# Branch and output projections of a hybrid decoder step: eight block products replaced by seven, with resident split weights and GpSimd sums

## The reference

```python
    h = h * jax.nn.sigmoid(o_pre) * jax.nn.silu(z_m)
    y_m = h @ w_proj_m
    cv, conv1 = short_conv(c_g * x_c, conv0, conv_w)
    y_c = (jax.nn.silu(z_c) * b_g * cv) @ w_proj_c
    mix = jax.nn.sigmoid(g_m) * y_m + jax.nn.sigmoid(g_c) * y_c
    out = x + mix @ w_out
```

## Time and profile before

| | |
|---|---|
| median of 3 runs (lowest, highest) | 2363.55 us (2358.3, 2364.69) |
| profiled execution, span from first to last instruction | 2356.7 us |
| TensorE busy | 2323.1 us, 99% |
| VectorE, ScalarE, GpSimd busy | 1488.1, 948.6, 77.5 us |
| mean granted TensorE clock | 0.998 |

### The profile page before, as it was taken

One profiled execution on the slowest core, in us unless ns is written; L12 is line 12 of the kernel. 1 busy time (PEld: TensorE's weight loads), 2 busy tenths in 40 slices (PEclk: granted clock), 3 DMA queues, 4 the chain that ended last, 5 costly groups with the idle time before them and its releaser, 6 DMA issues. The chain is left out here.

```text
span 2356.7 us, 41040 instructions
## 1 busy us (share of the span) xinstructions
PE 2323.1 (99%) x14643; PEld 2254.8 (96%) x14643; DVE 1488.1 (63%) x2703; ACT 948.6 (40%) x1717; POOL 77.5 (3%) x84
## 2 busy tenths in 40 slices
PE   8999999999999999999999999999999999999998
PEld 8998999999999999999999999999998999998886
DVE  4447788898876687777776677777755333324333
ACT  3224444444454444455655444555554101002121
POOL 0011000000110000000020000000000000000000
PEclk9999999999999999999999999999999999999999
DMA  6665655455775765656765766557567433443442
GB/s 224 209 215 136 199 187 181 157 177 176 232 220 174 232 202 184 191 159 195 240 191 177 235 202 195 188 175 217 176 185 260 156 102 110 138 143 126 138 138 86
DMA packets 424977, 425.66 MB, mean 181 GB/s; under 512 B 32810, under 2 KB 363690, under 8 KB 424870
## 3 DMA queue, kind: packets, MB, share of 16 engines
q1 hardware_dynamic: 424870, 424.25, 56.9%
HBM read 297.36 MB, written 126.85 MB: 180 GB/s over the span
## 5 line engine op out<-in xcount | busy, mean ns | idle before, releaser
L1658 PE MATMUL b_g<-x_hi,w_hi 128*128 128x344 f32 (+1 forms) x3024 | 985.5, 326 | 9.0 <-DVE rows L1333 4.3
L1658 PE MATMUL b_g<-x_lo,w_hi 128*128 128x344 f32 (+1 forms) x3024 | 967.9, 320 | 0.0
L1658 PE MATMUL b_g<-x_hi,w_lo 128*128 128x344 f32 (+1 forms) x3024 | 967.0, 320 | 0.0
L1658 PEld LDWEIGHTS b_g<-x_hi,w_hi 128*128 128x128 f32 x3024 | 569.3, 188 | 16.1 <-DVE rows L1333 4.4
L1658 PEld LDWEIGHTS b_g<-x_lo,w_hi 128*128 128x128 f32 x3024 | 569.3, 188 | 1.7
L1658 PEld LDWEIGHTS b_g<-x_hi,w_lo 128*128 128x128 f32 x3024 | 569.4, 188 | 0.0
L1155 ACT ACTIVATE w_hi<-w_operands 128x512 fp32r<-128x512 f32 x519 | 323.5, 628 | 272.9 <-PE b_g L1658 261.2
L1295 DVE TENSOR_TENSOR w_lo<-w_operands,w_hi 128x512 fp32r<-128x512 f32 x519 | 354.2, 695 | 1.2
L1155 ACT ACTIVATE w_hi<-stages 128x512 fp32r<-128x512 f32 x216 | 134.7, 629 | 138.3 <-PE b_g L1658 119.4
L1295 DVE TENSOR_TENSOR w_lo<-stages,w_hi 128x512 fp32r<-128x512 f32 x216 | 145.6, 684 | 7.7 <-ACT w_hi L1155 6.9
L2017 PE MATMUL c_g<-act_hi,RH 128*128 128x294 f32 x448 | 134.4, 300 | 2.1 <-DVE rows L1948 2.1
(11 more groups left out here) (305 smaller groups left out, 3116.0 us busy)
## 6 DMA issues: line engine op xcount, KB each, us to landing
w_operands<-w_in SPq DMA_DIRECT2D x282, 256.0 KB, 5.2
stages<-w_ops_d SPq DMA_DIRECT2D x36, 768.0 KB, 5.5
w_operands<-w_ops_d SPq DMA_DIRECT2D x34, 768.0 KB, 4.9
stages<-w_in SPq DMA_DIRECT2D x72, 256.0 KB, 3.8
w_operands<-w_ops_d SPq DMA_DIRECT2D x70, 256.0 KB, 6.3
w_ops_d<-w_operands SPq DMA_DIRECT2D x18, 768.0 KB, 3.3
w_ops_d<-stages SPq DMA_DIRECT2D x18, 768.0 KB, 3.4
w_ops_d<-w_operands SPq DMA_DIRECT2D x36, 256.0 KB, 3.9
```

Of the source, the lines that this page charges most:

```text
L1658: last = nc.tensor.matmul(bank[:, 0:n], w[:, j, k, :], x[:, k, 0:n], start=(j < 4 and k == 0 and m == 0), stop=(k == 3 and m == 2), skip_g ...
```

## The change

`phase_c` and `phase_d` are rewritten to the seven-product scheme. In `phase_c` the unit is a *pair*: one quarter `p` (of 4) of the output channels, as two blocks of 128 (`p` and `p`+4), times one tile of 2 x 258 tokens. 2 branches x 4 tiles x 4 quarters give 32 pairs, numbered n = 16 x branch + 4 x tile + p. A pair has 7 products, each 4 x 3 matmuls of 258 columns. Each pair alternates between two sets of four banks; products 5, 6 and 7 go on top of banks 0, 2 and 3 after ScalarE or VectorE has read them.

The weights are 12 *blocks* (4 quarters of each matrix). A block is loaded raw (`load_raw`, four transfers of 256 KB), three operands are sums (four instructions, `weight_sum`), and it is split in four pieces (`COARSE`; seven for the first and last block, `FINE`) by `split_high` on ScalarE and `split_low` on VectorE. Four blocks are resident (`WH`, `WL`), block b in slot b % 4. `AHEAD` says in which pair a block is split, `RAW_AT` in which its load is issued. `POOL_SUMS` is all of `AHEAD`: GpSimd makes the sums of all blocks but the first (made by VectorE at the end of `phase_b`) and, in its own block of code, of the last one. There is one raw buffer and one buffer for sums for blocks 0 to 8.

The activations of a tile are loaded as four quarters, GpSimd makes four sums (`act_sum`, 1032 elements a partition), ScalarE and VectorE split seven operands (`act_high`, `act_low`) during the last pair of the tile before. A pair's result is 128 x 2 x 516: ScalarE and VectorE gather it from PSUM (`step`) and one VectorE instruction applies the gate (`gate`). Branch m is stored to `mix_d`; branch c is added to it in DRAM by accumulating transfers which GpSimd issues (`accumulate`). `head_norm_w` is now multiplied into the z row in `phase_b`. `phase_d` takes tiles of 256 tokens with 84 matmuls of 512 columns, and the 8 samples in 48 matmuls with plain quarters of the same weights. The old bodies of both phases are left out here:

```diff
...
-TN = 294
-NTC = 7
-TP = TN * NTC
+TN = 258
+NG = 4
+TP = 2 * TN * NG
+NPAIR = 4 * NG * 2
+NT2 = L // (2 * P)
+STORED = [0, 4, 1, 5, 2, 3, 6]
+COARSE = [(2, 4), (0, 2), (4, 6), (6, 7)]
+FINE = [(0, 1), (4, 5), (1, 2), (5, 6), (2, 3), (3, 4), (6, 7)]
+SUMS_OF = {(0, 1): 0, (4, 5): 2, (1, 2): 3, (5, 6): 1, (2, 3): 0, (3, 4): 0, (6, 7): 4, (2, 4): 0, (0, 2): 3, (4, 6): 2}
+NW = 12
+BANK = (0, 1, 2, 3, 0, 2, 3)
...
+def load_raw(eng, g, b):
+    w, c0, c1 = weight_block(g, b)
+    w = w[0].rearrange("(k p) n -> p k n", p=P)
+    for j, (k0, c) in enumerate(((0, c0), (0, c1), (4, c0), (4, c1))):
+        eng.dma_start(raw_buffer(g, b)[:, j], w[:, k0:k0 + 4, c:c + P]).then_inc(raw_signal(g, b)[0], 16)
+def weight_sum(eng, engine, g, b, at):
+    r, e = raw_buffer(g, b), sum_buffer(g)
+    if at == 0:
+        engine.wait_ge(*raw_signal(g, b))
+        if b:
+            engine.wait_ge(g.w_ready, pieces_before(b))
+        eng.tensor_tensor(e[:, 1], r[:, 1], r[:, 3], ALU.add).then_inc(g.w_sum, 1)
+    elif at == 1:
+        engine.wait_ge(g.w_sum, 4 * b + 1)
+        eng.tensor_tensor(e[:, 0], e[:, 1], r[:, 0], ALU.subtract).then_inc(g.w_sum, 1)
+    elif at == 2:
+        eng.tensor_tensor(r[:, 1], r[:, 0], r[:, 1], ALU.subtract).then_inc(g.w_sum, 1)
+    else:
+        engine.wait_ge(g.w_sum, 4 * b + 2)
+        eng.tensor_tensor(e[:, 2], r[:, 2], e[:, 0], ALU.subtract).then_inc(g.w_sum, 1)
...
+def split_high(nc, act, g, b, at):
+    lo, hi = chunks(b)[at]
+    act.wait_ge(*raw_signal(g, b))
+    if SUMS_OF[lo, hi]:
+        act.wait_ge(g.w_sum, 4 * b + SUMS_OF[lo, hi])
+    nc.scalar.activation(g.WH[:, b % 4, lo:hi], piece(g, b, lo, hi), ACT.Copy).then_inc(g.w_hi, 1)
+def split_low(nc, dve, g, b, at):
+    lo, hi = chunks(b)[at]
+    dve.wait_ge(g.w_hi, pieces_before(b) + at + 1)
+    nc.vector.tensor_tensor(g.WL[:, b % 4, lo:hi], piece(g, b, lo, hi), g.WH[:, b % 4, lo:hi].bitcast(F32),
+                            ALU.subtract).then_inc(g.w_ready, 1)
...
+def act_sum(nc, pool, g, s, at):
+    a, b, c, d, e = (act_block(g, s, slot) for slot in range(5))
+    if at == 0:
+        pool.wait_ge(*act_signal(g, s))
+        if s:
+            pool.wait_ge(g.x_ready, 7 * s)
+        nc.gpsimd.tensor_tensor(b, c, b, ALU.subtract).then_inc(g.xq_sum, 1)
+    elif at == 1:
+        pool.wait_ge(g.xq_sum, 4 * s + 1)
+        nc.gpsimd.tensor_tensor(d, b, a, ALU.add).then_inc(g.xq_sum, 1)
+    elif at == 2:
...
-                        nc.scalar.activation(ZT[:, 0:n], ER[:, q, 1, 0:n], ACT.Tanh, scale=0.5).then_inc(z_set, 1)
+                        nc.scalar.activation(ZT[:, 0:n], ER[:, q, 1, 0:n], ACT.Tanh, scale=0.5)
+                        nc.scalar.activation(ER[:, q, 1, 0:n], ER[:, q, 1, 0:n], ACT.Copy,
+                                             scale=g.hnw[:, bass.ds(2 * i + q, 1)]).then_inc(z_set, 1)
...
+                        if extra == "end" and q == 1 and 2 <= j < 6:
+                            weight_sum(nc.vector, dve, g, 0, j - 2)
...
+    AHEAD = {0: 1, 1: 2, 2: 3, 13: 4, 14: 5, 16: 6, 17: 7, 29: 8, 30: 9, 31: 10}
+    RAW_AT = {0: 1, 1: 2, 2: 3, 4: 4, 14: 5, 15: 6, 17: 7, 18: 8, 28: 9, 30: 10, 31: 11}
+    POOL_SUMS = {n: b for n, b in AHEAD.items()}
...
+            def raw_weights(b):
+                if b <= 8:
+                    sp.wait_ge(g.w_ready, pieces_before(b - 1) + (2 if b > 1 else 6))
+                elif b == 10:
+                    sp.wait_ge(g.w_ready, pieces_before(8) + 2)
+                elif b == 11:
+                    sp.wait_ge(g.w_ready, pieces_before(9) + 2)
+                load_raw(sp, g, b)
+            load_tanh(0)
+            raw_weights(1)
...
+            for n in range(NPAIR):
+                s = n // 4 + 1
+                if n:
+                    load_tanh(n)
+                    if n <= NPAIR // 2:
+                        store(n - 1)
+                if n == 1:
+                    for par in range(2):
+                        sp.wait_ge(g.row_out[par], g.rows_stored[par])
+                if n % 4 == 0:
+                    sp.wait_ge(g.x_ready, 7 * s)
+                    if s == 2 * NG:
+                        for par in range(2):
+                            sp.wait_ge(g.acc_out[par], 32)
+                    load_acts(sp, g, s)
+                if n in RAW_AT and n:
...
+            def accumulate(n):
+                pool.wait_ge(gated, n + 1)
+                pool.dma_start(two_rows(g.mix_d, n), MX[n % 2], accum_op=ALU.add).then_inc(g.acc_out[n % 2], 16)
+            for n in range(NPAIR):
+                if n == NPAIR // 2:
+                    for par in range(2):
+                        pool.wait_ge(mix_out[par], 16 * NPAIR // 4)
+                if n > NPAIR // 2:
+                    accumulate(n - 1)
+                if n % 4 == 2:
+                    act_sum(nc, pool, g, n // 4 + 1, 0)
+                    act_sum(nc, pool, g, n // 4 + 1, 1)
+                if n in POOL_SUMS:
+                    for at in range(4):
+                        weight_sum(nc.gpsimd, pool, g, POOL_SUMS[n], at)
+                if n % 4 == 3:
+                    act_sum(nc, pool, g, n // 4 + 1, 2)
+                    act_sum(nc, pool, g, n // 4 + 1, 3)
+            accumulate(NPAIR - 1)
...
+            for j in range(NOP):
+                split_high(nc, act, g, 0, j)
+                act_high(nc, act, g, 0, j)
+                if j == 3:
+                    for br in range(2):
+                        row = g.ER[:, 1, br, 0:2 * PASSES[2][1]]
+                        nc.scalar.activation(row, row, ACT.Tanh, scale=0.5).then_inc(last_tanh, 1)
+            def step(n, j):
+                act.wait_ge(done, 7 * n + j + 1)
+                bank = G[4 * (n % 2)][:, 0:TN]
+                if j == 0:
+                    if n:
+                        act.wait_ge(ev, 5 * (n - 1) + 1)
+                    nc.scalar.activation(P1[:, :], bank, ACT.Copy).then_inc(copied, 1)
+                elif j == 4:
+                    row_free(act, n)
+                    nc.scalar.activation(MX[n % 2][:, 0, 0:TN], bank, ACT.Copy).then_inc(copied, 1)
+            for n in range(NPAIR):
+                for j in range(NOP):
+                    step(n, j)
+                    if n in AHEAD and j >= 3:
+                        split_high(nc, act, g, AHEAD[n], j - 3)
+                    if n % 4 == 3:
+                        act_high(nc, act, g, n // 4 + 1, j)
...
+            def gate(n):
+                dve.wait_ge(ev, 5 * n + 5)
+                dve.wait_ge(copied, 2 * n + 2)
+                dve.wait_ge(tg_in, 16 * (n + 1))
+                nc.vector.scalar_tensor_tensor(out=MX[n % 2], in0=TG[:, :, :], scalar=1.0, in1=MX[n % 2],
+                                               op0=ALU.add, op1=ALU.mult).then_inc(gated, 1)
+            def ahead(b, at):
+                if at in (2, 3) and b not in POOL_SUMS.values():
+                    weight_sum(nc.vector, dve, g, b, 2 * at - 4)
+                    weight_sum(nc.vector, dve, g, b, 2 * at - 3)
+                elif 4 <= at < 7:
+                    split_low(nc, dve, g, b, at - 4)
+                elif at == 7:
+                    split_low(nc, dve, g, b, 3)
+            for j in range(NOP):
+                split_low(nc, dve, g, 0, j)
+                act_low(nc, dve, g, 0, j)
+            for n in range(NPAIR):
+                for j in range(NOP):
+                    if j == 0:
+                        if n - 1 in AHEAD:
+                            ahead(AHEAD[n - 1], 7)
+                        if n and n % 4 == 0:
+                            act_low(nc, dve, g, n // 4, NOP - 1)
+                        if n:
+                            gate(n - 1)
+                    step(n, j)
+                    if n in AHEAD:
+                        ahead(AHEAD[n], j)
+                    if n % 4 == 3 and j:
+                        act_low(nc, dve, g, n // 4 + 1, j - 1)
+            gate(NPAIR - 1)
+            ahead(AHEAD[NPAIR - 1], 7)
+            act_low(nc, dve, g, 2 * NG, NOP - 1)
...
+            for n in range(NPAIR):
+                br, t, p = place(n)
+                for j in range(NOP):
+                    if t == 0:
+                        pe.wait_ge(g.w_ready, pieces_for(4 * br + p, j))
+                    if p == 0:
+                        pe.wait_ge(g.x_ready, 7 * (n // 4) + j + 1)
+                    if j == 0 and n > 1:
+                        pe.wait_ge(copied, 2 * (n - 1))
+                    elif j == 1 and n > 1:
+                        pe.wait_ge(ev, 5 * (n - 2) + 1)
+                    elif j == 2 and n > 1:
+                        pe.wait_ge(ev, 5 * (n - 2) + 4)
+                    elif j == 3 and n > 1:
+                        pe.wait_ge(ev, 5 * (n - 2) + 5)
+                    elif j == 4:
+                        pe.wait_ge(copied, 2 * n + 1)
+                    elif j == 5:
+                        pe.wait_ge(ev, 5 * n + 2)
+                    elif j == 6:
```

(8 more changed lines are left out.)

721 lines of the change are left out of this document (354 added, 367 removed).

## The result

| | before | after |
|---|---|---|
| median of 4 runs of each | 2361.03 us | 2440.52 us |
| lowest to highest | 2358.3 to 2364.69 | 2439.87 to 2443.41 |
| profiled execution, span | 2356.7 us | 2438.9 us |

The ratio is 1.0339 (95% interval 1.0325 to 1.0354): the changed kernel is slower by 79.5 us, where +16 was forecast and +38 was the range's end. Sign right, size wrong by a factor of five.

What follows compares the result with a forecast made beforehand. TensorE, busy 99% of the span, was taken as the bound. With waits the pair stage goes from 374.9 to 413.3 us (+38.4), the output stage saves 22.3: +16, a median of 2380 us, range 2350 to 2402.

Steps and rivals of the forecast that it cites:

- Tile changes 1.6 each: Pair stage, pairs 8, 12, 20, 24, 28: the sixth product waits for VectorE's second PSUM sum, 8 us together.
- the sides allow it: Output stage: VectorE's work fits beside each 19.5 us tile, so 96 fewer matmuls save the full 22.3 us.
- The first pairs: Pair stage's start: pairs 1 to 3 wait for weight loads, sums and splits; pair 4 starts at 83.0 us.
- Then 8.4 for the load: Pairs 2 and 3: tanh rows, a mix store and a weight block queued together need 8.4 us with their issues.
- Pairs 14 to 18: Pair stage: blocks 5 and 7 load in the pair that splits them, GpSimd holds block 6's sums; 21.8 us lost.
- barrier 0.8: Between pair and output stages: 0.8 us for the barrier, within 15.1 from the last pair matmul's end to the next.
- Pair 31 itself loses 1.8: Last pair of the pair stage: a loss of 1.8 us, counted beside the 15.1 us border.
- Costed at nothing: Input stage: z row scaling on ScalarE (24 copies, about 0.7 us each) and first block's sums (4 x 0.6) add nothing.
- Rivals 1: Pair stage: GpSimd's blocking costs almost nothing and waits are shorter; -14 us for the kernel, chance 0.24.
- 4: Rival with full gain, all weight block turnarounds hidden: -68 us over both stages, chance 0.02, counted within the faster rival's.
- rival 2: Whole kernel: gain and waits both halve, time within 0.3% (7 us) of before; chance 0.15.
- Rival 3: Pair stage from pair 18: accumulating transfers over 13 us hold up row buffers; at 16 us +21 more, chance 0.09.

Runs made afterwards that it cites:

- e1: Changed kernel with the output stage's activation loads issued one tile earlier on SP, ahead of the load of x and the store; 2421.9 us.
- e9: Changed kernel with raw blocks 1 to 3 and 5 to 7 loaded where their low parts will stand, and blocks 5 to 7 split later; 2402.2 us.
- e13: e9 with GpSimd's weight sums ahead of its wait for branch m's stores and of the accumulating transfer; 2390.2 us.
- e5: Changed kernel with GpSimd's sums for a pair, from pair 4 on, waiting until TensorE has finished the pair before; 2436.7 us.
- e3: Changed kernel with the last accumulating transfer issued as GpSimd's first instruction of the output stage, behind the barrier; 2436.4 us.
- e11: Changed kernel without the scaling of the z rows by the head norm weight (24 ScalarE copies); 2436.6 us, one run.
- e6: Changed kernel with the first weight block's four sums behind the last product of the last input pair on VectorE; 2439.9 us.
- e12: Changed kernel with the edits of e1, e3 and e9 together, all weight sums and the pair stage's activation sums on VectorE; 2334.1 us.
- e8: Changed kernel with weight sums and activation sums (all but the first block's and first group's) on VectorE instead of GpSimd; 2394.1 us.
- e14: e12 with the weight sums of blocks 1 to 11 back on GpSimd, ahead of the accumulating transfers; 2339.2 us.
- e7: Changed kernel with all 16 accumulating transfers made plain stores by the same queue; 2433.8 us, one run.
- e10: Changed kernel with only the activation sums (all but the first group's) on VectorE, weight sums staying on GpSimd; 2412.8 us.

## Why the prediction was wrong

**Right by its steps.** Starts of 258-column matmuls 0.120 us apart and of 512-column ones 0.233 (medians). Low parts beside GpSimd 3 us and more (up to 4.2). Tile changes 1.6 each: 1.9 (pairs 8, 24, 28), though pair 4, a tile change too, was left out of the list (1.8). VectorE ends 12.1 us after the last pair matmul: 12.3.

**The step that failed most** is "the sides allow it: a tile lasts 19.5 us, VectorE's part is ... 12 us, plus 5 us of blocking". It weighs VectorE's work against the tile and never follows when the next tile's activations land. 17 us of work in 19.5 doesn't fit if 6.8 us of it is spent before a load, with the needed sum behind it. The stage took 196.9 us for 176.1, 20.8 more; with the load early it takes 175.8 (e1). It is the largest term, and alone would have put the forecast at +37.

**The first pairs: right mechanism, partly by luck.** Pairs 1 to 4 at 28.5, 47.4, 71.2, 83.0: measured 29.3, 53.2, 75.4, 88.2. "Then 8.4 for the load" was mis-sized: block 2 landed 11.3 us after the gate of pair 0, block 3 10.1 us after that of pair 1. (The 11.4 us from which the 8.4 is worked out is a median; the transfer of the earlier trace rows itself took 11.8, with a fourth one issued behind it.) And the two activation sums that the prediction puts in front of block 3's ran earlier, beside block 2's low part:
```profile
1838.38 3.44 DVE L254 TENSOR_TENSOR proj_lo<-stages,proj_hi 128x1024 fp32r<-128x1024 f32 x1 [3.19 <-ACT proj_hi L248]
```
So pair 2 comes 5.0 us later than forecast and pair 3, counted from pair 2, 1.6 us earlier: part of the nearness of 75.4 to 71.2 is two errors that cancel.

**Pairs 14 to 18: right mechanism, size off.** "Gate of pair 13 at 1.9, so block 5 has landed at 10.3": the gate ended 6.9 us into pair 14, the block landed at 17.9. GpSimd's activation sums, written for pair 14 and begun 3.3 us before it, held up block 4's low parts (3.2 and 3.1 us for 1.2), and the load took 11.0 us from the gate, not 8.4. Pair 15 lost 15.5 and not 7.5. The reading that GpSimd holds the next sums until the stores have landed was right (e9, e13).

**GpSimd's order taken for its time.** The prediction lets a sum happen in the pair for which it is written. GpSimd has no other work and runs ahead: block 4's sums, written for pair 13, met the low parts of pair 11 (5.7 us at pair 12, e5).

**"VectorE ends 12.1 us after the last matmul; barrier 0.8":** the barrier took 5.9, for the last transfer (e3: 0.3 without it). **"Pair 31 itself loses 1.8":** it lost 6.6. TensorE stood there behind the copy and the second sum of its own pair:
```profile
2213.31 0.39 PE L2166 MATMUL c_g<-act_hi_b,proj_hi 128*128 128x258 f32 x1 [2.18 <-ACT c_part L2057]
2217.32 0.58 PE L2166 MATMUL c_g<-act_hi_b,proj_hi 128*128 128x258 f32 x1 [1.73 <-DVE c_part L2086]
```
The prediction had seen that GpSimd's sums stand there behind an accumulating transfer, and priced it too low: with them ahead of it pair 31 loses 0.1 us (e13, from 6.1 in e9). **"Costed at nothing"** were the z copies (about 3 us, e11, one run; ScalarE's idle share is an average and doesn't say what waits behind a copy) and the first block's sums, hidden as work but not as a wait for their load (3 us, of which e6 shows that it only moves).

**The clock was priced once, and is paid at each wait.** After the 8.79 us wait in pair 15, timeline of TensorE:
```profile
2015.33 0.42 PE L2166 MATMUL c_g<-act_hi_b,proj_lo 128*128 128x258 f32 x1
2015.55 0.42 PE L2166 MATMUL c_g<-act_hi_b,proj_hi 128*128 128x258 f32 x1
2015.77 0.42 PE L2166 MATMUL c_g<-act_lo_b,proj_hi 128*128 128x258 f32 x1
2015.98 0.42 PE L2166 MATMUL c_g<-act_hi_b,proj_lo 128*128 128x258 f32 x1
```
The starts are 0.215 us apart, not 0.120: the low one (1.2 GHz) of the two levels. Summed over TensorE's timeline, 217 matmuls of the pair stage ran so, for 21.2 us beyond the waits themselves (86.4 us), and 8.0 us in the output stage. In e12 it is 7.2 us beside 23.0 of waits, and 2.3. So a us of wait in the changed kernel's pair stage cost about 1.25 us; the forecast had 1.6 us of this in all, at pair 4. The Trainium skill (TensorE: Matmul & The Clock Gate, Back-to-back issue gap) has N/1.2 ns for a gap at this level, 215 ns at 258 columns, an estimate that the trace matches, unlike that page's figure for the high level, which the prediction weighed (110 ns; 120 measured).

**Rivals.** Rivals 1 (shorter waits) and 4 were wrong in sign, and rival 2 (no change to speak of) is out. Rival 1's objection, that a chain followed by counts waits twice, was wrong in kind: it leaves waits out. That blocking by GpSimd is real stands in e5 and e8, as the Trainium skill (SBUF — State Buffer, Who interferes with whom) has it: a VectorE instruction with two SBUF inputs contends with GpSimd's reads. The rows agree: low parts of 1.2 us take up to 4.2, sums from PSUM keep 0.41. For the weight sums it is one part, 3 to 10 us (e14), and their place in GpSimd's queue another (e13). Rival 3's transfers stayed under its 13 us, but the forecast's "so I take nothing" isn't borne out: see e7 and pair 31.

**Left open:** why the activation sums on VectorE alone shorten the border by 4.5 us (e10), and both kinds by 2.5 (e8; of the 4.5, 1.4 are only moved, since pair 31 loses 8.0 us in e10 for 6.6); why the load of a block lands 10.1 to 11.3 us after a gate; and the first 1800 us, where the same code starts its matmuls up to 5 us earlier or later from kernel to kernel, so that the parts of e3, e5 and e6 are read from the stages and not from the medians.

## What to carry to other kernels

Cost a stage not by an engine's work against the time, but by what stands behind each wait: for every load, follow its place in the issuing queue, its landing, the first instruction that waits for it on each in-order engine, and what stands behind that. One reordering of SP's queue gave 21 us, one of GpSimd's 10 to 12. An engine with little to do doesn't work where its code is written but as soon as it may, or stands before a transfer of its own while others need its next result. And once TensorE waits often, add what it loses after each wait at the low clock level.

## What was not expected of the hardware

- The barrier at a stage's end waited for GpSimd's own last transfer: 6.6 us from issue to release, with the landing at 6.3 (4.0 and 3.6 for a plain store, e7), and 0.3 us from VectorE's last instruction when there was none (e3).
- A 512-element sum on GpSimd stretches too when VectorE works beside it, 1.28 to 2.3 us: both lose, where the prediction had VectorE alone wait, and a sum moved there can cost VectorE more (0.8 us on a low part of 1.2) than it takes off it (0.69).
- An accumulating transfer of 516 KB issued by GpSimd landed 8.5 us after its issue in the median, against 7.2 for a plain store by the same queue (e7, one run) and 6.5 for the plain stores of branch m's rows issued by SP.
